# Gathering expert inputs from one token tile at a time, with slots numbered per tile

## What is computed

```python
h = rms_norm(x, norm2_g) * (1.0 + scale2) + shift2           # t: 256 tokens x 1024
scores = sigmoid(t @ w_router)                               # 64 experts
biased = scores + router_bias
...                                                          # 4 of 8 groups, then the 8 best experts of each token
w = w / sum(w) * 2.5
gu = einsum('cd,edf->cef', tc, w_experts_gate_up)            # 1024 -> 2 x 256 for each expert
act = silu(gu[..., :256]) * gu[..., 256:] * cc[..., None]
routed = einsum('cef,efd->cd', act, w_experts_down)          # 256 -> 1024
out = x + gate2 * (routed + shared)
```

## Time and profile before

| | us |
|---|---|
| median of 3 runs | 731.45 |
| lowest to highest | 729.86 to 733.39 |
| profiled execution, its own time | 729.72 |
| its span (first to last instruction) | 727.9 |
| PE busy in the span | 665.2 (91%) |
| DVE busy | 303.9 (42%) |
| ACT busy | 165.3 (23%) |
| POOL busy | 34.1 (5%) |
| mean granted clock of PE | 0.981 of full |

### The profile page before, as it was taken

How to read it: one execution, slowest core, us unless ns; L and a number is a source line. 1 busy time by engine, 2 the same in 40 slices (tenths; PEclk the granted TensorE clock), 3 DMA queues, 4 the chain that set the end, 5 groups by cost and what they waited for, 6 DMA issues and landing times.

```text
span 727.9 us, 10005 instructions
## 1 busy us (share of the span) xinstructions
PE 665.2 (91%) x3371; PEld 375.5 (52%) x3371; DVE 303.9 (42%) x690; ACT 165.3 (23%) x292; POOL 34.1 (5%) x61
## 2 busy tenths in 40 slices
PE   2899999999999999989999988989989998899895
PEld 0478866888785487653434433434333433343342
DVE  2338989988233386342222223122231222213314
ACT  2010133213220241122322312123221322222211
POOL 7001111000000001000000000000000000000001
PEclk9999999999999999999999999999999999999997
DMA  8999989633410007526899999999999999999961
GB/s 303 387 387 324 390 306 341 243 128 128 172 64 0 1 3 302 218 93 255 341 429 422 427 423 427 431 425 426 427 422 429 425 426 429 422 430 420 427 289 58
DMA packets 43132, 225.65 MB, mean 310 GB/s; under 512 B 3488, under 2 KB 3520, under 8 KB 29414
## 3 DMA queue, kind: packets, MB, share of 16 engines
q1 hardware_dynamic: 41528, 224.43, 76.5%
q10 hardware_dynamic: 1582, 0.94, 0.5%
HBM read 224.31 MB, written 1.05 MB: 310 GB/s over the span
## 4 chain that ended last, share of the span: by engine, by line
PE 56%; DMA 34%; SPq 3%; DVE 3%; issue 1%; ACT 1%; ACTq 0%; DVEq 0%
DMA raw<-n_w_experts_gate_up_dram 31%; PE bank L1149 16%; PE bank L1483 13%; PE bank L1432 4%; PE bank L1288 4%; PE bank L1320 4%; PE bank L1467 3%; DMA ring<-in_w_in_dram 3%; PE bank L1177 2%; SPq L319 2%; PE bank L1473 1%; SPq L323 1%; PE bank L1491 1%; PE bank L1100 1%; PE bank L1400 1%
## 5 line engine op out<-in xcount | busy, mean ns | idle before, releaser
L1149 PE MATMUL bank<-work,ring 128*128 128x256 f32 x512 | 116.1, 384 | 1.7 <-DMA ring<-in_w_in_dram 1.7
L1483 PE MATMUL bank<-raw,hT 128*32 128x512 f32 x832 | 96.9, 619 | 19.7 <-DMA raw<-n_w_experts_gate_up_dram 19.7
L1149 PEld LDWEIGHTS bank<-work,ring 128*128 128x128 f32 x512 | 97.3, 192 | 17.3 <-issue 2.9
L1467 PE MATMUL bank<-raw,hT 128*128 128x512 f32 x224 | 101.6, 607 | 2.8 <-ACT hT L629 2.8
L1048 DVE TENSOR_TENSOR sg<-sg,bank 128x256 f32<-128x256 f32 x27 | 11.4, 421 | 169.8 <-ACT sg L638 169.8
L1483 PEld LDWEIGHTS bank<-raw,hT 128*32 128x32 f32 x832 | 30.6, 114 | 84.7 <-issue 84.7
L1467 PEld LDWEIGHTS bank<-raw,hT 128*128 128x128 f32 x224 | 42.1, 193 | 62.1 <-issue 60.4
L1443 PE MATMUL bank<-y,ST 128*128 128x512 f32 x224 | 71.0, 440 | 2.3 <-DVE y L1057 2.3
L1473 PE MATMUL bank<-raw,aT 128*128 128x512 f32 x112 | 51.7, 604 | 8.7 <-ACT aT L643 8.7
L647 ACT ACTIVATE y<-bank,wcol 128x512 fp32r<-128x512 f32 x54 | 34.1, 683 | 108.5 <-PE bank L1473 54.3
L638 ACT ACTIVATE sg<-bank 128x256 f32<-128x256 f32 x27 | 17.1, 634 | 182.4 <-PE bank L1483 99.2
(11 more groups left out here) (279 smaller groups left out, 582.3 us busy)
## 6 DMA issues: line engine op xcount, KB each, us to landing
raw<-n_w_experts_gate_up_dram SPq DMA_DIRECT2D x53, 2048.0 KB, 16.7
raw<-in_w_experts_down_dram SPq DMA_DIRECT2D x53, 1024.0 KB, 18.5
ring<-in_w_ada_dram SPq DMA_DIRECT2D x12, 2048.0 KB, 18.5
ring<-in_w_in_dram SPq DMA_DIRECT2D x9, 2048.0 KB, 13.1
ring<-in_w_out_dram SPq DMA_DIRECT2D x2, 2048.0 KB, 8.5
ring<-in_w_attn_out_dram SPq DMA_DIRECT2D x1, 2048.0 KB, 19.0
ring<-in_w_conv_out_dram SPq DMA_DIRECT2D x1, 2048.0 KB, 7.7
ring<-in_w_shared_gate_up_dram SPq DMA_DIRECT2D x1, 2048.0 KB, 7.9
```

The lines of the kernel that those rows point to most:

```text
L1149: ins = mm(b[:, kk * SEQ:(kk + 1) * SEQ], w[:, k, m * PART:(m + 1) * PART], h1T[:, k, :], start=(k == 0), stop=(k == KD - 1))
L1467: ins = mm(psU[:, :], hT[:, k, :], wg[:, k, :], start=(k == 0), stop=(k == KD - 1))
L1483: ins = mm(psU[c:c + 32, :], hT[:, k, c:c + 32], w_gu(s)[:, k, :], start=(k == 0), stop=(k == KD - 1))
```

## The change

Slots are numbered in two ranges: 0 to 1023 for token tile 0, 1024 to 2047 for tile 1 (each tile has 128 x 8 = 1024). An expert now has two pieces in `hs`, one in each range. So each block of 512 slots needs only one token tile: two matmuls for a block of channels in place of four, one product (L1437 in the changed kernel) and one comparison for a selection in place of two. `hT` is twice as wide. An expert's input is made by two copies: the window that starts at its first slot in the low range, and then, once `hT_low` says that this has landed, the window of the high range, written `split_at` columns to the right. So ACT loads three numbers for each expert (low, high, split) in place of one. ACT's `aT` copy moves ahead of the next input (`turned`). The table's entries for experts and offsets are made first (`experts_ready`, on which SP now waits for its first load), those for the starts later (`tabs_ready`). The turned slot numbers come straight from matmuls with `before` (whose diagonal now holds 4096), in place of two transposes. Scatter and down are as before.

```diff
-    T_START, T_EXP = 2, 2 + CAND
+    T_EXP, T_OFF, T_LOW, T_HIGH, T_SPLIT = (2 + CAND * i for i in range(5))
+    SELECTED = 4096.0
+    TILE = PART * TOPK
...
-        hT = sb("hT", [PART, KD, PART])
+        hT = sb("hT", [PART, KD, 2 * PART])
...
         BIG, MID, SMALL = 1, 2, (0, 3)
-        TRIO_COLS = [(MID, 0), (MID, 32), (SMALL[0], 64), (SMALL[1], 96)]
-        TRIO_WINDOWS = [(MID, 0, 64), (SMALL[0], 64, 32), (SMALL[1], 96, 32)]
+        TRIO_COLS = [(MID, 0, 0), (MID, 32, 32), (SMALL[0], 64, 128), (SMALL[1], 96, 192)]
...
 
-        def window_of(engine, j):
-            return engine.value_load(tab[0:1, bass.ds(j + T_START, 1)], min_val=0, max_val=SLOTS)
+        def offset_of(engine, j):
+            return engine.value_load(tab[0:1, bass.ds(j + T_OFF, 1)], min_val=0, max_val=PART)
+
+        def windows_of(engine, j, n):
+            low = engine.value_load(tab[0:1, bass.ds(j + T_LOW, 1)], min_val=0, max_val=TILE)
+            high = engine.value_load(tab[0:1, bass.ds(j + T_HIGH, 1)], min_val=TILE, max_val=SLOTS)
...
             sp.wait_ge(*users[WOUT + 1])
-            sp.wait_ge(tabs_ready, 1)
+            sp.wait_ge(experts_ready, 1)
...
 
-            def big_input(g):
-                p = window_of(a, g)
-                a.activation(hT[:, :, :], hs[:, :, bass.ds(p, PART)], ACT.Copy).then_inc(hT_ready, 1)
-
-            def trio_input(g):
-                for s, c, n in TRIO_WINDOWS:
-                    p = window_of(a, trio_rank(s, g, n_big, n_trio))
-                    ins = a.activation(hT[:, :, c:c + n], hs[:, :, bass.ds(p, n)], ACT.Copy)
+            def input_of(windows, i):
+                wins = [(at, n) + windows_of(a, j, n) for j, at, n in windows]
+                for at, n, low, high, split_at in wins:
+                    ins = a.activation(hT[:, :, at:at + n], hs[:, :, bass.ds(low, n)], ACT.Copy)
+                ins.then_inc(hT_low, 1)
+                a.wait_ge(hT_low, i + 1)
+                for at, n, low, high, split_at in wins:
+                    ins = a.activation(hT[:, :, bass.ds(split_at + at, n)], hs[:, :, bass.ds(high, n)], ACT.Copy)
                 ins.then_inc(hT_ready, 1)
+
+            def big_input(g, i):
+                input_of([(g, 0, PART)], i)
+
+            def trio_input(g, i):
+                input_of([(trio_rank(s, g, n_big, n_trio), at, n) for s, c, at, n in TRIO_WINDOWS], i)
 
             def gate():
                 a.activation(sg[:, :].rearrange("s (k f) -> s f k", k=KF), psU[:, 0:F].rearrange("s (f k) -> s f k", k=KF),
                              ACT.Silu).then_inc(silu_done, 1)
 
-            def outputs(i, down, count):
+            def turned(i):
                 a.wait_ge(t_done, i + 1)
                 a.activation(aT[:, :, :], psM[:, 0:F].rearrange("p (k n) -> p k n", k=KF), ACT.Copy).then_inc(aT_ready, 1)
+
+            def outputs(i, down, count):
                 a.wait_ge(down, count)
                 a.wait_ge(st_ready, i + 2)
                 for n in range(2):
                     a.activation(y2[:, 0, n * W:(n + 1) * W], psY[n][:, :], ACT.Copy, scale=wcol[:, 0:1]).then_inc(y_hi, 1)
 
...
                 gate()
-                trio_input(g)
+                turned(g * 2)
+                trio_input(g, g * 2 + 1)
                 outputs(g * 2, big_dn, g + 1)
                 a.wait_ge(trio_gu, g + 1)
                 gate()
-                big_input(g + 1)
+                turned(g * 2 + 1)
+                big_input(g + 1, g * 2 + 2)
                 outputs(g * 2 + 1, trio_dn, g + 1)
             with a.Fori(n_trio, n_big) as g:
                 a.wait_ge(big_gu, g + 1)
                 gate()
-                big_input(g + 1)
+                turned(g + n_trio)
+                big_input(g + 1, g + n_trio + 1)
                 outputs(g + n_trio, big_dn, g + 1)
 
...
-            v.tensor_scalar(perm, iota[:, 0:CAND], rank, None, ALU.is_equal)
+            v.tensor_scalar(perm, iota[:, 0:CAND], rank, None, ALU.is_equal).then_inc(perm_ready, 1)
+            v.tensor_scalar(split_at, ecnt[:, 0:1], offc[:, 0:1], 0.0, ALU.subtract, ALU.max)
+            link(v.tensor_scalar(skipped, ecnt[:, 0:1], offc[:, 0:1], 0.0, ALU.subtract, ALU.min))
+            link(v.scalar_tensor_tensor(skipped, left, 0.0, skipped, ALU.is_gt, ALU.mult))
             v.wait_ge(ecum_done, 1)
-            link(v.tensor_scalar(startv, bank[3][:, 448:449], offc[:, 0:1], -float(SLOTS), ALU.add, ALU.add))
-            v.scalar_tensor_tensor(startv, left, 0.0, startv, ALU.is_gt, ALU.mult).then_inc(tabs_ps_in, 1)
-            v.tensor_copy(ecum, bank[3][0:E, 448:449])
-            link(v.tensor_copy(cnt, bank[0][:, 128:128 + E]))
-            link(v.tensor_tensor_scan(incl, ones[:, 0:E], cnt, 0.0, ALU.mult, ALU.add))
-            link(v.tensor_tensor(first, incl, cnt, ALU.subtract))
-            v.wait_ge(tabs_ps, 1)
-            v.tensor_scalar(tab[0:1, T_START:T_START + CAND], bank[7][0:1, 0:CAND], float(SLOTS), None, ALU.add)
-            v.tensor_copy(tab[0:1, T_EXP:T_EXP + CAND], bank[7][0:1, CAND:2 * CAND]).then_inc(tabs_ready, 1)
-            link(v.tensor_tensor(slotm[:, :, :], bank[3][:, 256:256 + TH * E].rearrange("p (t e) -> p t e", t=TH),
-                                 first.unsqueeze(1).broadcast_to([PART, TH, E]), ALU.add))
-            link(v.scalar_tensor_tensor(slotm[:, :, :], slotm[:, :, :], 1.0, r["sel"], ALU.add, ALU.mult))
-            v.tensor_scalar(slotm[:, :, :], slotm[:, :, :], -1.0, None, ALU.add).then_inc(slotT_out, 1)
-            link(v.tensor_tensor(eend, ecum, ecnt[0:E, :], ALU.add))
-
-            def emat(q):
-                qs = slice(q * W, (q + 1) * W)
-                link(v.tensor_scalar(Emat[:, qs], iota[0:E, qs], eend[:, 0:1], None, ALU.is_ge))
-                v.scalar_tensor_tensor(Emat[:, qs], iota[0:E, qs], ecum[:, 0:1], Emat[:, qs].bitcast(fp32),
+            link(v.scalar_tensor_tensor(firsts, ecnt, -SELECTED, bank[3][:, 448:450], ALU.mult, ALU.add))
+            v.scalar_tensor_tensor(high, firsts[:, 1:2], float(TILE), skipped, ALU.add, ALU.subtract).then_inc(starts_in, 1)
+            v.wait_ge(experts_ps, 1)
+            v.tensor_copy(tab[0:1, T_EXP:T_EXP + 2 * CAND], bank[7][0:1, 0:2 * CAND]).then_inc(experts_ready, 1)
+
+            def slots_turned(t):
+                v.tensor_scalar(slotT[:, t * PART:(t + 1) * PART], bank[3][0:E, t * PART:(t + 1) * PART],
+                                firsts[0:E, t:t + 1], -SELECTED, ALU.add, ALU.add).then_inc(slotT_ready, 1)
+
+            slots_turned(0)
+            link(v.tensor_tensor(ends, firsts[0:E, :], ecnt[0:E, :], ALU.add))
+
+            def emat(b):
+                t, at = divmod(b, 2)
+                bs, js = slice(b * W, (b + 1) * W), slice(at * W, (at + 1) * W)
+                link(v.tensor_scalar(Emat[:, bs], iota[0:E, js], ends[:, t:t + 1], None, ALU.is_ge))
+                v.scalar_tensor_tensor(Emat[:, bs], iota[0:E, js], firsts[0:E, t:t + 1], Emat[:, bs].bitcast(fp32),
                                        ALU.is_ge, ALU.subtract).then_inc(E_ready, 1)
 
-            v.wait_ge(slotT_ps, 1)
-            v.tensor_copy(slotT, bank[3][0:E, 0:SEQ])
             emat(0)
+            v.wait_ge(starts_ps, 1)
+            v.tensor_copy(tab[0:1, T_LOW:T_LOW + 3 * CAND], bank[7][0:1, 0:3 * CAND]).then_inc(tabs_ready, 1)
+            slots_turned(1)
+            v.tensor_scalar(slotm[:, :, :], bank[3][:, 256:256 + TH * E].rearrange("p (t e) -> p t e", t=TH),
+                            -SELECTED, None, ALU.add).then_inc(slotm_ready, 1)
             h2_lo(1)
...
+            def select(b):
+                v.wait_ge(m1_done, b + 1)
+                if b >= 2:
+                    v.wait_ge(gather_ps, KD * (b - 1))
+                at = (b % 2) * W
+                v.tensor_tensor(SS[:, b % 2, :], bank[M1_B[b]][:, :], iota[:, at:at + W], ALU.is_equal).then_inc(SS_ready, 1)
...
-            pe.wait_ge(tabs_ps_in, 1)
-            mm(bank[7][0:1, 0:CAND], startv, perm, start=True, stop=True)
-            mm(bank[7][0:1, CAND:2 * CAND], expc[:, :], perm, start=True, stop=True).then_inc(tabs_ps, 1)
+            pe.wait_ge(perm_ready, 1)
+            mm(bank[7][0:1, 0:CAND], expc[:, :], perm, start=True, stop=True)
+            mm(bank[7][0:1, CAND:2 * CAND], offc[:, :], perm, start=True, stop=True).then_inc(experts_ps, 1)
             shared_up(0, 3, range(4, KD))
-            pe.wait_ge(slotT_out, 1)
-            for t in range(TH):
-                ins = tr(bank[3][0:E, t * PART:(t + 1) * PART], slotm[:, t, :], ident[:, :])
-            ins.then_inc(slotT_ps, 1)
+            pe.wait_ge(starts_in, 1)
+            pe.wait_ge(experts_ready, 1)
+            for i, col in enumerate((firsts[:, 0:1], high, split_at)):
+                ins = mm(bank[7][0:1, i * CAND:(i + 1) * CAND], col, perm, start=True, stop=True)
+            ins.then_inc(starts_ps, 1)
...
+            for b in range(4):
+                pe.wait_ge(SS_ready, b + 1)
+                if b % 2 == 0:
```

(49 more changed lines are left out.)

86 lines of the change are left out of this document (39 added, 47 removed).

## The result

| | before | changed |
|---|---|---|
| median, us | 732.21 (4 runs) | 770.85 (4 runs) |
| lowest to highest | 729.86 to 733.39 | 768.47 to 772.94 |
| span of the profiled execution | 727.9 | 768.2 |
| mean granted clock of PE | 0.981 | 0.942 |

The ratio is 1.0531, with a 95% interval from 1.0507 to 1.0555: the change makes the kernel slower by 5.3%. The forecast was 771.

What follows compares the result with a forecast made beforehand. Bound: expert weights by DMA in the loop, PE in the gather. Terms +0.9 - 9.8 + 2.3 + 27.6 + 19.2 + 0.3 = +40.5 us on 729.72 give 770.2; the median, 1.7 us above, 771 us; range 749 to 789.

Steps and rivals of the forecast that it cites:

- Routing: Before the gather: six small matmuls more and two fewer on PE delay the first gather result, +0.9 us.
- Gather: Half the matmuls per result; copies out of the banks become the bound, 31.7 us against 41.4, -9.8 us.
- First input: Between gather and first big gate/up: ACT makes three loads and two copies, not one each, +2.3 us.
- Late inputs: Loop: nine loads behind ACT's `aT` copy make PE wait for a trio's input, 31.2 us a pair against 29.5, +27.6 us.
- E: In the loop: the time at which PE's big gate/up of a round ends.
- Clock: Trio gate/ups: PE's clock falls behind about 4.4 us idle time, 12 of 13 times 1.6 us, +19.2 us.
- The end: After the last trio gate/up: the last big input comes later, +0.3 us.
- the loads that run ahead of the wait: Rival, ACT's queue: loads run while the `aT` copy waits, loop stays bound by weights, 725 us; chance 0.06.
- The rival in which the clock holds: Trio gate/ups: the clock's fall stays rare or short, 752 us (743 to 758); chance 0.20.
- The rival in which the gather gains nothing: Gather: evictions and selections queue on DVE or the clock falls, 781 us; over 789 us, with other causes, chance 0.05.

Runs made afterwards that it cites:

- the filled wait: Changed kernel plus four unused fp32 matmuls on PE between the big round's down and the wait for the trio's input; 743.61 us, ratio 1.0167.
- the third bank: Changed kernel with table loads ahead of ACT's wait for PE's gate/up, plus gather results rotating over three PSUM banks, not two; 720.03 us, ratio 0.984.
- the early loads: Changed kernel with the next input's table loads made before ACT's wait for PE's gate/up, not behind the `aT` copy; 724.91 us, ratio 0.9897.
- the run with twelve loads: Changed kernel with three more, unused table loads on ACT ahead of each trio's nine; 791.97 us, one run.
- nine loads, three copies: Changed kernel with all nine loads and the `hT_low` wait, but a one-column copy in place of the high copies; 747.85 us, one run.

## Why the prediction was right, and where its terms were off

The forecast of 771 us met 770.85, but two of its terms were wrong by 10 and 8 us with opposite signs. The path that it named was the right one; that the number came out to 0.2 us is luck. In the order of its parts, by the chain and timeline above:

- **Routing, +0.9 us; measured +2.6.** From the start of the last mixer product to the first gather record are 54.07 us before, 56.66 changed. 1.5 us of the difference are the clock, which no part had reckoned with in this place: it was low from 273 to 277 us, and two groups of small matmuls took 1.84 and 2.01 us in place of 1.16.

```profile
272.00:274.00 2.00, 2.00 (x17) 1.92 (x17) 1.79 (x10) 0.00 (x0) 0.66 (x3) 0.82 0.00 0
274.00:276.00 2.00, 2.00 (x11) 1.74 (x11) 0.30 (x2) 0.16 (x1) 0.61 (x4) 0.50 0.00 0
276.00:278.00 2.00, 2.00 (x15) 1.57 (x14) 0.56 (x2) 0.00 (x0) 1.30 (x6) 0.83 0.00 0
```

In the run with the filled wait the clock held here, and the same distance was 55.14 us, +1.07 for the chain itself.

- **Gather, -9.8 us; measured -10.0.** From 283.39 to 315.00 are 31.6 us against 41.6. That the copies would be the bound is shown by the third bank.
- **First input, +2.3 us; measured +2.1**, 4.12 us from the last copy to PE's start in place of 2.06. The first gate/up behind this longer wait took 9.77 us in place of 8.84, which was not in the sum. The loop starts 5.5 us earlier; 6.6 were forecast.
- **Late inputs, +27.6 us; measured +17.4.** From the end of the first big gate/up, 328.89, to that of the last trio, 738.42, are 409.5 us; less the 27.6 of the clock below, and against 364.55 before, that is 17.4. The mechanism was the forecast one, shown by the early loads. Its size was too large: the input of a trio lets PE start at E + 10.13, not 10.6, and from the end of a trio gate/up to the big one are 6.15 us as before, not 6.4. A pair without the clock is 30.4 us (10.13 + 7.07 + 6.15 + 7.06), not 31.2; the run with the filled wait shows 30.39. The loads cost what was reckoned: the low copies start at E + 7.4. Three neighbouring copies then take 1.25 us in place of 1.5, and PE starts 0.04 us behind the last one in place of 0.2.
- **Clock, +19.2 us; measured +27.6.** The 13 trio gate/ups take 119.54 us in the chain, 13 times 7.07 are 91.9. I had taken 12 of 13 at 1.6 us, from waits of 2.35 us. (The seven waits that it counted are six of 2.35 to 2.39 us, three of them followed by the low clock, and one of 3.15 us, which was not.) All 13 were slow, and in turn by 1.5 and by 2.6 us: the wait of 4.1 us costs more, not only more often. A still longer one costs no more, 119.1 us in all behind the 5.7 us of the run with twelve loads. The filled wait gave 27.2 us back.
- **The end, +0.3; measured -0.1.** The sum of what was measured is -5.5 + 0.9 (the longer first gate/up) + 17.4 + 27.6 - 0.1 = 40.3, as between the spans.

Of the rivals, the loads that run ahead of the wait did not happen in the changed kernel's order, and are just what the early loads bring by hand: 724.9 us, where that rival had 725. The rule of the Trainium skill ("Perfetto Trace Analysis", section on the DVE / Act engine instruction), that the sequencer goes on once a waiting instruction is in the wait queue, is not borne out here for loads of table entries behind an activation that waits: they started after it, in both kernels. The rival in which the clock holds, 752 us, did not come about; where the filled wait made it hold, the kernel took 743.6 us, 8.4 us lower, mainly because the late inputs had been overrated by 10 us. The rival in which the gather gains nothing is refuted by its 10.0 us.

## What to carry to other kernels

Count what an engine's queue has to do between a wait and the work that others need, and put loads whose addresses are long known ahead of the wait: here 0.6 us each, nine times, turned a gain into a loss of 5%. Where a loop is bound by DMA with 2 us to spare, everything on the other engines is free up to those 2 us, and then costs twice, since PE's clock falls behind the wait and this too is now on the path. When matmuls of an alternating pair of PSUM banks are halved, see whether the copies out of them become the bound before counting the gain.

## What was not expected of the hardware

Behind the waits of 4.1 us each all 13 gate/ups ran partly at the low clock, and their lengths alternated strictly between 8.57 and 9.7 us; with 2.95 us (nine loads, three copies) all 13 were slow too, by 1.5 us and more, while behind the 2.37 us waits for weights only some were. In the run with early loads six waits for weights took 3.27 to 3.30 us: three of the gate/ups behind them took 8.4 to 10.0 us, three 7.07. And behind 5.7 us (the run with twelve loads) all 13 were slow, but by 1.7 to 2.2 us and without the alternation. So the length of a wait alone does not tell whether the clock falls or for how long it stays low; what else sets this was not tried. In the routing, with PE busy almost without a break but with small matmuls only, the clock fell to 1.2 GHz in six of the eleven profiled executions (0.50 from 274 to 276 us in the changed kernel) and stayed up in the other five (1.00 throughout with the filled wait). That cost 1.5 us, and what decides between the two is open.
